# Sixteen more modulation steps placed after the recurrence, in three buffers, and attention's output projection begun in held banks

## The chip, the cores and the metric

The kernel runs on one core of one Trainium2 chip, as one launch. The metric is the device time of that core in microseconds, the median of several executions. Before the change three executions took 1273.87, 1274.51 and 1278.54 us, so the median is 1274.51 us.

## What is computed

One step of a two-layer streaming encoder over a prompt of 256 rows and a sample of 64 rows, each row 1024 wide, 320 columns together in the kernel's transposed layout. Cut to what matters:

```python
for l in range(2):
    mod = silu(c) @ ada_w[l] + ada_b[l]            # 1024 x 6144, one row per sequence
    sh1, sc1, g1, sh2, sc2, g2 = split(mod, 6)
    if l == 1:
        kvsh, kvsc = split(silu(c) @ kv_ada_w + kv_ada_b, 2)      # 1024 x 2048
        k, v = split(modulate(rmsnorm(x), kvsh, kvsc) @ w_kv)     # shared keys and values
    h = modulate(rmsnorm(x), sh1, sc1)
    y = rwkv7_time_mix(h) if l == 0 else window_attn(h, k, v)     # both end in a 1024 x 1024 projection
    x = x + g1 * y
    h = modulate(rmsnorm(x), sh2, sc2)
    x = x + g2 * hier_moe(h)                       # 32 experts of 1024 x 512 and 256 x 1024
y = rmsnorm(x)
```

The modulation vectors depend on `c` alone, so nothing but their first use says when they must be computed.

## The kernel before

The engines' programs are written by hand, each in its own order, with semaphores between them; a helper `Engine` counts what each engine did, and `wait` waits for a named piece of another engine's work. Nothing reorders: what stands later in an engine's program, or in SyncE's list of loads, can't overtake. All matmuls of a kind go through the helper `mm` (line 697), so most TensorE rows of the profile have that line.

**Modulation.** `MODS` (line 150) lists six groups of 2048 columns of `ada_w` or `kv_ada_w` beside the first one. A group is eight steps of 128 input rows; a step needs a load of 128 x 2048 values (1 MB), and is four matmuls of 512 columns against `cs` (`mod_rows`), which add up in one PSUM bank that is held over the group (`Banks.hold`, line 227). After the eighth step ScalarE copies the bank to a row buffer, TensorE transposes it (`mod_turn`, line 709), and VectorE adds the bias (`turned`, line 1564). Steps 0 to 31 (`EARLY = 4` groups, `MSTEPS = 32`) stand in the recurrence, steps 32 to 47 in attention (`late_step`, line 733). SyncE loads them in turn into two buffers (`mw`, `mw_late`), a load waiting until the step two before it has used its buffer.

**Recurrence** of layer 0 (time mixing), in chunks of 64 columns, 5 chunks. Part A (from line 889 on) computes per chunk the 64 x 64 products, and turns `v`, `b`, `k` to rows; one modulation step stands after the products and two after the turning (`A_STEPS = 3`). Then `for l in range(2, 7)` (line 914) inverts triangular matrices by five levels of doubling: per level five `W` products, then per chunk one `TW` product, which VectorE (lines 1707 to 1719) masks, adds and transposes, and which the next level's `W` needs. After the `TW` of chunks 0, 1, 2, 3 one modulation step each (`LEVEL_STEPS`, line 155). Then the state recursion, the normalisation of `y` (`head_sums`, `head_spread`), and the output projection `wo` (line 1006): eight outputs of eight matmuls each, whose inputs VectorE delivers one chunk at a time ("mix out").

**Prelude of the experts** (`moe`, line 1008): mean square, `keep_busy` (matmuls on constants into an unused bank), router logits, turning, ranks, gathering of rows; then a loop over the experts. SyncE's list in `moe_loads` (line 512) fills the ring's four slots.

**Attention** of layer 1 (loop at line 1242): stages s = 0 to 10 pipeline eight chunks; `project("q", [s])`, two late modulation steps, `mod_turn`, `prob_turn(s-3)`, `q_turn(s-1)`, `scores(s-2)`, `attended(s-3)`. In the tail (s = 8 to 10) there is no `q` and no modulation step. Then `project("ao", range(C), ...)` (line 1264) makes the eight outputs, then the second prelude and the second expert loop.

PSUM has eight banks, given out in turn by `Banks.open` (line 233), which leaves out held banks and waits until the bank's last owner has been read:

```python
        while self.n % 8 in self.held:
            self.n += 1
        ...
        if self.owner[b] is not None:
            self.pe.wait("read", *self.owner[b])
```

Of the kernel before, what the change touches and what calls it, by code (L numbers as in the profile page):

```python
# [36 lines left out]
P = 128  # L37
# [114 lines left out]
EARLY = 4  # L152
MSTEPS = C * EARLY
A_STEPS = 3
LEVEL_STEPS = (1, 1, 1, 1, 0)
# [89 lines left out]
def build(nc, i, o, known, seen):  # L245
    ctx = ExitStack()
    with ctx:
# [3 lines left out]
        def sem(name):  # L251
# [30 lines left out]
                                       "swkv_in", "router_in0", "router_in1", "out_written", "modw_in0", "modw_in1", "lora2_in")}  # L282
# [112 lines left out]
        modrow = [ring[:, 3 * B + 2048:3 * B + 2560], work[:, 6 * B:6 * B + 512]]  # L395
        mw_late = [ring[:, s_ * SLOT + 4096:(s_ + 1) * SLOT] for s_ in (2, 3)]
        modrow_late = work[:, 7 * B + 2048:8 * B]
# [87 lines left out]
        def _(eng):  # L485
# [25 lines left out]

            def moe_loads(l):
# [58 lines left out]
            def mod_load(n, dst):  # L571

                w, l, blk, _b = MODS[n // C]
                src = i[w] if l is None else i[w][l]
                eng.dma_start(dst, src[P * (n % C):P * (n % C) + P, 2048 * blk:2048 * (blk + 1)]
                              ).then_inc(in_sems[f"modw_in{n % 2}"], 16)

            for n in range(MSTEPS):
# [6 lines left out]
                mod_load(n, mw[n % 2])  # L585
# [10 lines left out]
            for n in range(MSTEPS, C * len(MODS)):  # L596
                if n >= MSTEPS + 2:
                    sp.wait("mod used", n - 2)
                mod_load(n, mw_late[n % 2])
# [91 lines left out]
        def _(eng):  # L691
# [17 lines left out]
            def mod_turn(g):  # L709
# [3 lines left out]
                for qd in range(4):  # L713
                    cols = slice(P * qd, P * qd + P)
                    ins = eng.transpose(pb[:, cols], (modrow_late if g >= EARLY else modrow[g < 0])[:, cols],
                                        ident)
                full(ins, "modT", g)

            def mod_step(n):
# [3 lines left out]
                if n < MSTEPS:  # L723
# [4 lines left out]
                    eng.wait_ge(in_sems[f"modw_in{n % 2}"], 16 * (n // 2 + 1))  # L728
                    pe.did(mod_rows(ps[seen_bank(("mod", g))], c, mw[n % 2]), ("mod used", n), ("mod", g))
# [3 lines left out]
            def late_step(n):  # L733
# [5 lines left out]
                eng.wait_ge(in_sems[f"modw_in{n % 2}"], 16 * (n // 2 + 1))  # L739
# [1339 lines left out]
```

## Time and profile before

| | |
|---|---|
| median of three runs | 1274.51 us |
| the profiled execution's own time | 1278.17 us |
| its span, first to last instruction | 1276.4 us |
| mean granted TensorE clock | 0.952 of full speed |
| TensorE matmul busy | 1130.6 us (89%) |
| VectorE busy | 541.1 us (42%) |
| ScalarE busy | 341.3 us (27%) |
| HBM read | 293.77 MB, 232 GB/s over the span |

The profiled execution is 3.66 us above the median, and its span 1.77 us below its own time. In the rows, PE is TensorE, PEld its weight loads, DVE VectorE, ACT ScalarE, SP SyncE; times are in us from the span's start, and a float32 matmul appears as two rows' worth of instructions, so a step of four matmuls counts as x8. A number in brackets is the time for which the engine stood idle before the row, with what ended it.

### The profile page before, as it was taken

The page shows a single profiled execution, that of the slowest core. Times are in us where ns is not written, and L with a number is a line of the kernel's source. Part 1 is how long each engine was busy: PE and PEld are TensorE (multiplying, and loading weights), DVE is VectorE, ACT ScalarE, POOL GpSimd, SP SyncE. Part 2 cuts the span into 40 slices and gives each one's busy share as a digit, 9 for nine tenths or more (in the row PEclk, how much of TensorE's full clock was granted, in tenths as well). Part 3 has the DMA queues.
Part 4 walks back from the last instruction along what each step waited for, and adds up shares of the span by engine and source line. Part 5 has one row for each costly group of instructions (what it writes and reads, how often), then busy time and mean ns, then how long its engine had stood idle before and what let it go on. Part 6 is the DMA issues. An engine that isn't in the chain of part 4 may idle for free.

```text
span 1276.4 us, 22255 instructions
## 1 busy us (share of the span) xinstructions
PE 1130.6 (89%) x8975; PEld 652.7 (51%) x8975; DVE 541.1 (42%) x1419; ACT 341.3 (27%) x650; POOL 56.3 (4%) x66
## 2 busy tenths in 40 slices
PE   5579998888888799999999989898899999999984
PEld 2146666656686556444444446455666444444433
DVE  3430366544522545244444444144346244444434
ACT  1112241112123012233333222233222233333312
POOL 2000000000000000001000000000000000010000
PEclk9589999998999799999999999999899999999997
DMA  9631313875632440399999964457250199999931
GB/s 238 197 132 66 132 66 108 281 257 193 232 135 64 175 190 1 138 415 426 425 427 424 423 236 186 160 209 280 91 198 1 65 425 420 426 427 424 426 152 41
DMA packets 45971, 297.11 MB, mean 233 GB/s; under 512 B 5956, under 2 KB 7336, under 8 KB 22344
## 3 DMA queue, kind: packets, MB, share of 16 engines
q1 hardware_dynamic: 43856, 290.17, 57.3%
q0 software_dynamic: 1840, 5.79, 2.0%
q8 instruction: 58, 0.95, 0.3%
q10 hardware_dynamic: 200, 0.06, 0.0%
q14 instruction: 17, 0.14, 0.0%
HBM read 293.77 MB, written 2.24 MB: 232 GB/s over the span
## 4 chain that ended last, share of the span: by engine, by line
PE 78%; DVE 9%; DMA 8%; ACT 2%; issue 2%; SPq 0%; ACTq 0%; DVEq 0%; POOL 0%; POOLq 0%
PE bank L697 76%; DMA ring<-in_ada_w 6%; DVE work L1545 2%; ACT work L1286 1%; DMA ring<-in_kv_ada_w 1%; DVE work L1551 1%; DVE work L1548 1%; DVE rstd L1583 1%; DVE x_res L1917 1%; DMA ring<-in_rw_w_rkv 1%; PE bank L1095 1%; DVE work L1903 1%; DVE ring L1545 1%; DVE work L1657 0%; PE bank L1215 0%
## 5 line engine op out<-in xcount | busy, mean ns | idle before, releaser
L697 PE MATMUL bank<-ring,work 128*64 128x512 f32 (+1 forms) x1600 | 341.2, 579 | 9.3 <-DVE work L1903 7.6
L697 PE MATMUL bank<-work,ring 128*128 128x320 f32 (+3 forms) x1600 | 302.5, 367 | 24.0 <-DVE work L1545 8.4
L697 PEld LDWEIGHTS bank<-work,ring 128*128 128x128 f32 (+2 forms) x1600 | 213.1, 172 | 112.3 <-issue 25.2
L697 PE MATMUL bank<-work 128*128 128x320 bf16 (+7 forms) x1906 | 225.3, 284 | 21.9 <-DVE x_res L1917 7.7
L697 PEld LDWEIGHTS bank<-ring,work 128*64 128x64 f32 (+1 forms) x1600 | 112.9, 137 | 210.7 <-issue 203.6
L697 PEld LDWEIGHTS bank<-work 128*128 128x128 bf16 (+3 forms) x1906 | 165.6, 126 | 93.6 <-issue 25.8
L1286 ACT ACTIVATE work<-bank 128x320 f32<-128x320 f32 (+6 forms) x113 | 57.0, 540 | 244.2 <-PE bank L697 218.6
L1917 DVE SCALAR_TENSOR_TENSOR x_res<-bank,mod,x_res 128x256 f32<-128x256 f32 (+1 forms) x256 | 86.1, 378 | 18.5 <-PE bank L697 4.8
L1897 DVE SCALAR_TENSOR_TENSOR work<-work,small,bank 128x256 f32<-128x256 f32 x32 | 21.5, 672 | 168.7 <-ACT work L1450 89.3
L697 PE MATMUL bank<-ring,cs 128*32 128x512 f32 x448 | 63.3, 656 | 31.5 <-DMA ring<-in_ada_w 23.9
L697 PEld LDWEIGHTS bank<-ring 64*64 64x64 f32 (+2 forms) x1984 | 71.8, 140 | 26.0 <-issue 23.8
L697 PE MATMUL bank<-ring 64*64 64x64 f32 (+2 forms) x1984 | 82.1, 232 | 3.4 <-issue 3.4
L1286 ACT ACTIVATE ring<-bank 128x512 f32<-128x512 f32 (+3 forms) x65 | 36.5, 561 | 151.4 <-PE bank L697 150.3
L1910 DVE TENSOR_TENSOR work<-bank,work 128x512 f32<-128x512 f32 x64 | 44.0, 688 | 61.9 <-ACT work L1454 61.9
L651 POOL TENSOR_TENSOR work<-work 128x512 bf16<-128x512 f32 x32 | 36.4, 1158 | 538.2 <-ACT work L1458 538.2
L1454 ACT ACTIVATE work<-bank 128x512 bf16<-128x512 f32 x64 | 38.1, 595 | 49.3 <-PE bank L697 49.3
L1551 DVE SCALAR_TENSOR_TENSOR work<-work,vec 128x320 f32<-128x320 f32 x56 | 27.0, 546 | 54.5 <-PE bank L697 54.2
L1438 ACT COPY work<-work 128x512 f32 x64 | 39.3, 623 | 14.2 <-issue 14.1
L1458 ACT ACTIVATE work<-work 128x512 bf16<-128x512 f32 x64 | 40.0, 626 | 8.6 <-DVE work L1910 8.6
L1286 ACT ACTIVATE work<-x_res 128x640 f32<-128x640 f32 x20 | 14.7, 737 | 99.9 <-DVE x_res L1551 46.5
L697 PEld LDWEIGHTS bank<-ring,cs 128*32 128x32 f32 x448 | 10.5, 112 | 56.7 <-DMA ring<-in_ada_w 30.6
L697 PE MATMUL bank<-const 128*128 128x320 f32 x122 | 37.9, 466 | 0.0
(189 smaller groups left out, 801.8 us busy)
## 6 DMA issues: line engine op xcount, KB each, us to landing
ring<-in_moe_w_gu SPq DMA_DIRECT2D x64, 2048.0 KB, 13.8
ring<-in_moe_w_down SPq DMA_DIRECT2D x64, 1024.0 KB, 14.6
ring<-in_ada_w SPq DMA_DIRECT2D x40, 1024.0 KB, 5.3
ring<-in_rw_w_rkv SPq DMA_DIRECT2D x6, 2048.0 KB, 7.9
ring<-in_ada_w SPq DMA_DIRECT2D x4, 2048.0 KB, 29.5
ring<-in_kv_ada_w SPq DMA_DIRECT2D x8, 1024.0 KB, 5.4
ring<-in_rw_w_o SPq DMA_DIRECT2D x2, 2048.0 KB, 11.9
ring<-in_at_w_q SPq DMA_DIRECT2D x2, 2048.0 KB, 14.1
```

Source lines behind the costliest of these rows:

```text
L651: eng.tensor_tensor(dpart[:, 0, 2, cols], rest[:, n, :], dpart[:, 0, 1, cols], ALU.subtract).then_inc(S["lo_ready0"], 1)
L697: return eng.matmul(out, l, r, start=start, stop=stop, **kw)
L1095: ins = eng.transpose(ps[0][:, 2 * P * u + P * f:2 * P * u + P * f + P], hid[:, u, P * f:P * f + P], ident)
L1286: ac.did(eng.activation(out, in_, f, **kw), *keys)
L1438: eng.copy(xe[:, u, :, 64 * v:64 * v + 64], xall[:, :, bass.ds(at, SLOTS)]).then_inc(S["xe_ready"], 1)
L1454: eng.activation(dpart[:, u, 0, 512 * n:512 * n + 512], ps[4 + n][:, :], ACT.Copy).then_inc(S["hi_ready"], 1)
L1458: eng.activation(dpart[:, u, 1, 512 * n:512 * n + 512], rest[:, n, :], ACT.Copy).then_inc(S["mid_ready"], 1)
L1545: op(eng.tensor_tensor(out, a, b, o_), *keys)
L1551: op(eng.scalar_tensor_tensor(out, a, s_, b, o1, o2), *keys)
L1897: eng.scalar_tensor_tensor(hid_w[:, u], silu[:, u, :].rearrange("p (q f) -> p q f", f=2), wslot[:, u:u + 1], ps[3 + 4 * u][:, FE:2 * FE].r ...
L1910: eng.tensor_tensor(rest[:, n, :], ps[4 + n][:, :], dpart[:, u, 0, 512 * n:512 * n + 512], ALU.subtract).then_inc(S["rest_ready"], 1)
L1917: ins = eng.scalar_tensor_tensor(x[:, c, t0:t0 + n], ps[(6, 1, 2)[c % 3]][:, t0:t0 + n], mod[:, l, r, 40 + c:40 + c + 1], x[:, c, t0:t0 + ...
```

## The change

Steps 16 to 31 (groups 2 and 3: the shared keys' modulation, and shift and scale of layer 1) leave the recurrence, and `MIDDLE = 4` marks where they end. In the recurrence part A keeps two steps per chunk, and the levels two of four (after the `TW` of chunks 0 and 2), so that the sixteen that are left are done by level 4. Step 16 goes behind the sum of `yc` squares, step 17 behind the spread of `y rstd`, steps 18 to 25 behind one output each of `wo`, 26 to 28 and 29 to 31 into the first prelude, where `keep_busy` has 13 matmuls less (7, 9 and 6 become 1, 3 and 5). Their loads go into three buffers in `work`, and into SyncE's list at four places of `moe_loads(0)`. The third buffer is where `bonus` lay, so its first load waits for the last "mix out". A copy on ScalarE and two additions on VectorE per group move with them, and a memset of `xall`'s tail, whose place the buffers take, goes behind them.

In attention, three of the eight outputs of `ao` get banks that are held from stage 8 on; their partial products over chunks 0 to 3 stand at the head of stage 8, chunks 4 and 5 at the head of stage 9, chunk 6 behind the loop, chunk 7 inside the fourth output. The number of matmuls is the same.

```diff
-EARLY = 4
+EARLY = 2
 MSTEPS = C * EARLY
-A_STEPS = 3
-LEVEL_STEPS = (1, 1, 1, 1, 0)
+A_STEPS = 2
+LEVEL_STEPS = (1, 0, 1, 0, 0)
+MIDDLE = 4
...
+        mw_middle = [work[:, a:a + 2048] for a in (B, 3 * B, 2 * B)]
...
+            def middle_loads(steps):
+
+                for n in steps:
+                    if n == MSTEPS + 2:
+                        sp.wait("mix out", PAIRED[-1])
+                    elif n > MSTEPS + 2:
+                        sp.wait("mod used", n - 3)
+                    mod_load(n)
+
             def moe_loads(l):
...
                     sp.wait("y all")
+                    middle_loads(range(MSTEPS, MSTEPS + 2))
                     eng.wait_ge(in_sems["out_written"], 64)
                     moe_gu(l, 2, 2)
                     moe_dn(l, 2, 2)
                     moe_gu(l, 3, 3)
                     sp.wait("y rstd all", PAIRED[-1])
                     moe_dn(l, 3, 3)
+                    middle_loads(range(MSTEPS + 2, MSTEPS + 9))
                 for s in ((0, 1) if l == 0 else (0, 1, 3, 2)):
+                    if l == 0 and s == 1:
+                        middle_loads(range(MSTEPS + 9, MSTEPS + 13))
...
+                if l == 0:
+                    middle_loads(range(MSTEPS + 13, MSTEPS + 16))
...
             head_sums("yc sum", E[0], "yc squares")
+            late_step(MSTEPS)
             pe.wait("y rstd")
             head_spread("y rstd all", heads)
-            project("wo", range(C), rr, lambda hf: ("wo", hf), ("mix out",))
+            late_step(MSTEPS + 1)
+            for m in range(C):
+                project("wo", [m], rr, lambda hf: ("wo", hf), ("mix out",))
+                if m == C - 1:
+                    mod_turn(EARLY)
+                late_step(MSTEPS + 2 + m)
...
                 mean_square(f"B{l}")
-                keep_busy(7)
+                if l == 0:
+                    for n in range(MSTEPS + 10, MSTEPS + 13):
+                        late_step(n)
+                keep_busy(7 if l else 1)
...
-                keep_busy(9)
+                if l == 0:
+                    for n in range(MSTEPS + 13, MSTEPS + 16):
+                        late_step(n)
+                    bank.held.clear()
+                keep_busy(9 if l else 3)
                 pe.wait("mask", l)
...
-                keep_busy(6)
+                if l == 0:
+                    mod_turn(EARLY + 1)
+                keep_busy(6 if l else 5)
...
+            def out_part(cs_):
+
+                for m in range(3):
+                    if m not in part:
+                        arrived(pe, "ao", 0)
+                        part[m] = bank.hold("ao", m)
+                for c in cs_:
+                    pe.wait("oT", c)
+                    for m in range(3):
+                        ins = mm(part[m][:, 0:T], w512(3)[:, c, 128 * m:128 * m + 128], oT[:, c, :], c == 0,
+                                 c == C - 1)
+                        if c == C - 1:
+                            full(ins, "ao", m)
+
             for s in range(C + 3):
+                if s == C:
+                    bank.held.clear()
+                    out_part(range(4))
+                if s > C:
+                    out_part([4, 5] if s == C + 1 else [])
...
-            project("ao", range(C), oT, lambda hf: ("ao", hf), ("oT",))
+            out_part([6])
+            pb = bank.open("ao", 3)
+            for c in range(C):
+                if c == C - 1:
+                    out_part([c])
+                ins = mm(pb[:, 0:T], w512(3)[:, c, 384:512], oT[:, c, :], c == 0, c == C - 1)
+            pe.did(ins, ("ao", 3), ("used", "ao", 0))
+            bank.held.clear()
+            project("ao", range(4, C), oT, lambda hf: ("ao", hf), ("oT",))
...
             def squares(tag):
                 for b in range(4):
+                    if tag == "B0" and b == 2:
+                        act(modrow_of(EARLY), pk("mod", EARLY)[:, :], ACT.Copy, ("read", "mod", EARLY),
+                            ("mod rows", EARLY))
...
+                if l == 0:
+                    late_turned(EARLY + 1)
+                    ve.wait("mod used", C * MIDDLE - 1)
+                op(eng.memset(xall[:, :, ROWS:RP], 0.0))
```

The line numbers shift, so that `mm` is line 728 in the changed kernel, `mod_turn`'s transposes line 746, and `prob_turn`'s lines 1262 and 1267. In the rows of order, `x` counts the matmuls as they are written.

TensorE, one level of the doubling and the next level's start, in the kernel before (64x64 are the `W` and `TW` products, 16 each; `ring,cs` a modulation step):

```order
L697 MATMUL bank<-ring,cs 32x512 x4
L697 MATMUL bank<-ring 64x64 x112
L697 MATMUL bank<-ring,cs 32x512 x4
L697 MATMUL bank<-ring 64x64 x16
L697 MATMUL bank<-ring,cs 32x512 x4
L697 MATMUL bank<-ring 64x64 x16
L697 MATMUL bank<-ring,cs 32x512 x4
L697 MATMUL bank<-ring 64x64 x16
L697 MATMUL bank<-ring,cs 32x512 x4
L697 MATMUL bank<-ring 64x64 x112
```

and in the changed one:

```order
L728 MATMUL bank<-ring,cs 32x512 x4
L728 MATMUL bank<-ring 64x64 x128
L728 MATMUL bank<-ring,cs 32x512 x4
L728 MATMUL bank<-ring 64x64 x32
L728 MATMUL bank<-ring,cs 32x512 x4
L728 MATMUL bank<-ring 64x64 x128
```

Two of the four steps of a level have gone, and between the two that are left stand two `TW` products on one side, and on the other two `TW`, five `W` and one `TW`.

TensorE from the sum of `yc` squares to the first outputs of `wo`, in the kernel before (`ring,const_phase` is the spread, `work,ring` the projection's 64 matmuls):

```order
L697 MATMUL bank<-work,const 32x320 x8
L697 MATMUL bank<-ring,const_phase 128x320 x8
L697 MATMUL bank<-work,ring 128x320 x64
L697 MATMUL bank<-work,const 128x320 x8
L697 MATMUL bank<-const 128x320 x7
```

and in the changed one (`work,cs` is a modulation step from the new buffers), the first rows and the last ones:

```order
L728 MATMUL bank<-work,const 32x320 x8
L728 MATMUL bank<-work,cs 32x512 x4
L728 MATMUL bank<-ring,const_phase 128x320 x8
L728 MATMUL bank<-work,cs 32x512 x4
L728 MATMUL bank<-work,ring 128x320 x8
L728 MATMUL bank<-work,cs 32x512 x4
...
L728 MATMUL bank<-work,ring 128x320 x8
L746 MATMUL bank<-const,work 128x128 x4
L728 MATMUL bank<-work,cs 32x512 x4
L728 MATMUL bank<-work,const 128x320 x8
L728 MATMUL bank<-work,cs 32x512 x12
L728 MATMUL bank<-const 128x320
```

A step stands behind each output, and behind the last one also a turn, ahead of the mean square (`work,const 128x320`).

TensorE in attention from the last modulation step's stage on, with the banks' numbers, in the changed kernel (bank 3 was held by modulation group 5 until there; `work,ring 128x320` is the output's part):

```order
L728 MATMUL bank3<-ring,cs 32x512 x8
...
L728 MATMUL bank2<-work 64x64 x16
L728 MATMUL bank3<-work,ring 128x320
L728 MATMUL bank4<-work,ring 128x320
L728 MATMUL bank5<-work,ring 128x320
...
L1262 MATMUL bank6<-const,work 128x128 x4
L1267 MATMUL bank7<-const,work 64x128 x4
L728 MATMUL bank0<-work,const_phase 128x320
```

Between `attended(4)` (bank 2) and the turn of chunk 5's probabilities (bank 6), where nothing stood before, there are now twelve matmuls into banks 3, 4 and 5.

## Rows read from the trace of the kernel before

**Rows 1.** Page, part 4: the chain that ended last, by engine.
```profile
PE 78%; DVE 9%; DMA 8%; ACT 2%; issue 2%; SPq 0%; ACTq 0%; DVEq 0%; POOL 0%; POOLq 0%
```

**Rows 2.** Waits of TensorE, 205 to 470 us: total us, times, longest.
```profile
PE bank L697 <- DMA ring<-in_ada_w: 12.7, 9, 2.3
...
PE bank L697 <- DMA ring<-in_kv_ada_w: 6.5, 4, 2.1
```

**Rows 3.** Timeline of TensorE in the recurrence: start, duration, operation, idle before.
```profile
212.66 5.15 PE L697 MATMUL bank<-work,ring 64*64 64x128 f32 x64 [2.83 <-DVE work L1545]
...
224.88 3.71 PE L697 MATMUL bank<-work,ring 64*64 64x128 f32 x64
228.52 1.06 PE L697 MATMUL bank<-ring,cs 128*32 128x512 f32 x8
229.51 1.15 PE L697 MATMUL bank<-const,work 64*64 64x64 f32 x32
230.49 2.03 PE L697 MATMUL bank<-const,ring 64*64 64x64 f32 x64
...
235.33 1.07 PE L697 MATMUL bank<-ring,cs 128*32 128x512 f32 x8 [1.81 <-DMA ring<-in_ada_w]
...
271.94 5.81 PE L697 MATMUL bank<-ring 64*64 64x64 f32 x192
...
357.87 1.10 PE L697 MATMUL bank<-const,ring 64*64 64x64 f32 x32
```

**Rows 4.** Timeline of VectorE, the first two chunks of a level.
```profile
277.88 0.69 DVE L1545 TENSOR_TENSOR ring<-ring,const_phase 128x512 f32<-128x512 f32 x1 [9.34 <-PE bank L697]
278.49 0.68 DVE L1545 TENSOR_TENSOR ring<-ring,bank 128x512 f32<-128x512 f32 x1
...
279.88 0.69 DVE L1545 TENSOR_TENSOR ring<-ring,const_phase 128x512 f32<-128x512 f32 x1
```

**Rows 5.** Stretches: length; busy PE, PEld, DVE, ACT, POOL; granted clock; DMA share; GB/s.
```profile
259.00:262.00 3.00, 3.00 (x36) 2.45 (x30) 0.76 (x2) 0.00 (x0) 0.00 (x0) 0.67 0.90 300
...
889.00:893.00 4.00, 4.00 (x22) 2.90 (x24) 1.01 (x3) 1.19 (x2) 0.00 (x0) 0.50 0.96 406
893.00:897.00 4.00, 4.00 (x64) 3.10 (x60) 1.75 (x6) 0.76 (x5) 0.00 (x0) 0.76 1.05 446
...
888.88:909.04 20.16, 16.29 (x166) 12.49 (x166) 7.45 (x31) 8.50 (x30) 0.00 (x0) 0.67 0.57 239
909.04:945.23 36.19, 36.19 (x131) 25.46 (x130) 9.00 (x21) 2.65 (x4) 0.00 (x0) 0.96 0.22 87
```

**Rows 6.** Timelines of TensorE and VectorE around the output projection of layer 0.
```profile
416.42 1.97 PE L697 MATMUL bank<-ring,const_phase 32*128 32x320 f32 x16 [3.27 <-DVE ring L1734]
...
429.48 0.49 DVE L1545 TENSOR_TENSOR work<-work 128x320 f32<-128x320 f32 x1
432.03 0.68 DVE L1551 SCALAR_TENSOR_TENSOR x_res<-bank,mod,x_res 128x256 f32<-128x256 f32 x2 [2.06 <-PE bank L697]
436.34 0.68 DVE L1551 SCALAR_TENSOR_TENSOR x_res<-bank,mod,x_res 128x256 f32<-128x256 f32 x2 [3.63 <-PE bank L697]
```

**Rows 7.** Page, part 6: loads, count, KB each, median us to landing.
```profile
ring<-in_moe_w_gu SPq DMA_DIRECT2D x64, 2048.0 KB, 13.8
...
ring<-in_ada_w SPq DMA_DIRECT2D x40, 1024.0 KB, 5.3
```

**Rows 8.** First prelude: a wait of TensorE, and when the experts' first matmuls ran.
```profile
PE bank L697 <- DVE work L1824: 2.2, 1, 2.2
...
523.28 7.11 PE bank L697 x32
```

**Rows 9.** Timelines of attention's tail: TensorE, ScalarE, and VectorE's last output.
```profile
888.88 1.11 PE L1215 MATMUL bank<-const,work 128*128 128x128 f32 x4 [4.17 <-DVE work L1548]
...
887.10 0.62 ACT L1286 ACTIVATE work<-bank 128x512 f32<-128x512 f32 x1
...
945.23 0.80 DVE L1548 TENSOR_SCALAR work<-bank,mod,bog 128x256 f32<-128x256 f32 x2 [2.99 <-PE bank L697]
```

More of the change, by code:

```diff
@@ L394, in build, with modrow_of, mod_at @@
         mw = [ring[:, 3 * B:3 * B + 2048], ring[:, tail3:tail3 + 2048]]
-        modrow = [ring[:, 3 * B + 2048:3 * B + 2560], work[:, 6 * B:6 * B + 512]]
         mw_late = [ring[:, s_ * SLOT + 4096:(s_ + 1) * SLOT] for s_ in (2, 3)]
-        modrow_late = work[:, 7 * B + 2048:8 * B]
+        mw_middle = [work[:, a:a + 2048] for a in (B, 3 * B, 2 * B)]
+        modrows = {"first": work[:, 6 * B:6 * B + 512], "early": ring[:, 3 * B + 2048:3 * B + 2560],
+                   "middle": work[:, B + 2048:2 * B], "late": work[:, 7 * B + 2048:8 * B]}
+        def modrow_of(g):
+            return modrows["first" if g < 0 else "early" if g < EARLY else "middle" if g < MIDDLE else "late"]
+        def mod_at(n):
+            if n < MSTEPS:
+                return mw[n % 2], f"modw_in{n % 2}", 16 * (n // 2 + 1)
+            m = n - MSTEPS
+            if n < C * MIDDLE:
+                return mw_middle[m % 3], f"modm_in{m % 3}", 16 * (m // 3 + 1)
+            return mw_late[n % 2], f"modw_in{n % 2}", 8 * MSTEPS + 16 * ((n - C * MIDDLE) // 2 + 1)
         lows = {"w": ring[0:64, tail3:tail3 + T], "a": ring[64:128, tail3:tail3 + T],
@@ L595, in _ @@
                 half(name, w, hf)
-            for n in range(MSTEPS, C * len(MODS)):
-                if n >= MSTEPS + 2:
+            for n in range(C * MIDDLE, C * len(MODS)):
+                if n >= C * MIDDLE + 2:
                     sp.wait("mod used", n - 2)
-                mod_load(n, mw_late[n % 2])
+                mod_load(n)
             half(("ao", 1), i["at_w_o"][0], 1)
@@ L1302, in mod_copy @@
                     ac.wait("modT", g - 1)
-                    act(modrow[0], pb[:, :], ACT.Copy, ("read", "mod", g), ("mod rows", g))
+                    act(modrow_of(g), pb[:, :], ACT.Copy, ("read", "mod", g), ("mod rows", g))
             ac.wait("rows zeroed")
@@ L1321, in _ @@
             root("A0")
-            act(modrow[1], pk("mod", -1)[:, :], ACT.Copy, ("read", "mod", -1), ("mod rows", -1))
+            act(modrow_of(-1), pk("mod", -1)[:, :], ACT.Copy, ("read", "mod", -1), ("mod rows", -1))
             modulated("A0", h0, h0)
@@ L1423, in moe @@
                 act(rt[:, 36, 0:3], rt[:, 35, 0:3], ACT.Exp, ("route exp", l))
+                if l == 0:
+                    g = EARLY + 1
+                    pb = pk("mod", g)
+                    ac.wait("modT", EARLY)
+                    act(modrow_of(g), pb[:, :], ACT.Copy, ("read", "mod", g), ("mod rows", g))
                 for hf in range(2):
@@ L1507, in _ @@
                 if s in (4, C):
-                    g = EARLY + (s == C)
-                    act(modrow_late[:, :], pk("mod", g)[:, :], ACT.Copy, ("read", "mod", g), ("mod rows", g))
+                    g = MIDDLE + (s == C)
+                    act(modrow_of(g), pk("mod", g)[:, :], ACT.Copy, ("read", "mod", g), ("mod rows", g))
                 if s >= 3:
@@ L1757, in moe @@
                 eng.wait_ge(in_sems["out_written"], (64, 144)[l])
-                op(eng.memset(xall[:, :, ROWS:RP], 0.0))
                 op(eng.tensor_tensor_scan(count640[:, :], cst("ones")[:, 0:1].broadcast_to([P, ROWS]),
```

54 lines of the change are left out of this document (30 added, 24 removed).

## The prediction, made before the changed kernel was run

> **What bounds the kernel now.** I read the chain of waits first: 78% of the span it runs through TensorE, and 8% through DMA [rows 1]. So two questions decide this change: where does TensorE wait, and does moved work land where it waited anyway? TensorE's waits between 205 and 470 us give the first answer. It stood 12.7 and 6.5 us, 19.2 in all, for loads of modulation weights [rows 2], and all of that lies in the recurrence. The timeline shows how: a step is 0.99 us (228.52 to 229.51), with three per chunk, and the third finds its load not there (1.81 us at 235.33) [rows 3]. Next I read who is second: VectorE in the levels [rows 4]. Then the stretches that take the moved work: the projection of layer 0, where VectorE waits for TensorE 3.63 us per output [rows 6], so TensorE is the bound there, and attention's tail, where TensorE pauses 4.17 us in one piece [rows 9].
>
> **Part A of the recurrence.** A chunk without its waits is 3.64 us of products (224.88 to 228.52), 0.98 and 2.03 us of turning, and its steps [rows 3]. With two steps that is 3.64 + 0.98 + 2.03 + 1.98 = 8.6 us, so five chunks take 43.0; the first one's products take 1.4 longer (5.15 for 3.71), a turn 0.6: 45.0 us, for 271.94 - 212.66 = 59.3 now. **Minus 14.3.** Do the loads keep up? A buffer comes free when its step is done, and is wanted one chunk of 8.6 us less one step later, 7.6 us; a load lands after 5.3 us [rows 7]. They do.
>
> **The levels.** They take 357.87 - 271.94 = 85.9 us [rows 3]. Ten products of 16 x 2 instructions are 5.81 / 6 = 0.97 us each, 9.7 us a level; with two steps 11.7. VectorE needs 2.0 us per chunk (277.88 to 279.88), 10.2 a level at 2.05, and becomes second: after its fifth chunk's add (0.69 + 0.68 us in) the last `W` and the next `TW` must run, 1.94, and two hand-overs of some 0.2, while only 0.7 of transposing is left [rows 4]. So a level has a floor of 10.2 + 1.7 = 11.9 us on VectorE too. Taking 12.0: 5.8 to the first `TW`, four periods, four products: 5.8 + 48.0 + 3.9 = 57.7, which saves 28.2. I take 1.4 off for pauses in which TensorE waits for nothing shown, "issue", 2% of the chain [rows 1]. **Minus 26.8.** Bounds for the whole recurrence: at least the sixteen steps' own 16 us and half the load waits, 9.6, so 25.6; at most 14.3 + 28.2 = 42.5, where nothing is lost.
>
> **Where the steps go.** Steps 16 and 17 cost nothing: their loads start when `y` is done, and they run at about 413 and 418 us, where TensorE waits for VectorE's reciprocal (3.27 us at 416.42) and then for the inputs of `wo`, the last of which comes at 429.97 [rows 6]. Without that cover they would cost 2.0.
>
> Steps 18 to 25 stand between the outputs of `wo`, which follow each other at 4.31 us (432.03 to 436.34) on a full TensorE [rows 6]: nothing hides them. **Plus 8.0**, and the turn behind the last one **plus 0.6**.
>
> Step 18 has a new wait. Its buffer is `bonus`, so its load, and those of 19 and 20 behind it in SyncE's list, wait for the last "mix out" at 429.97 [rows 6], and land 5.3 us later, at 435.3 [rows 7]. Output 0 is done at 431.9, so TensorE stands 3.4 us with seven outputs queued behind the step. **Plus 3.4** (bounds: 0, if the load were as quick as the 2.06 us VectorE waits there; 11.9, if it took the 13.8 of an expert load with others ahead). The next loads have two periods, 10.6 us, and don't wait.
>
> The DMA page of the Trainium skill, "DMA: Bandwidth & Descriptors", section Bandwidth, gives 6.15 us for 1 MB, measured on the POOL queue; by it the stall would be 4.3 and the sum 0.9 more. The trace's 5.3 is of these loads on this queue, and decides.
>
> Such a pause also costs clock. After the longest of the waits for loads, 2.3 us [rows 2], the granted clock at 259 to 262 was 0.67; after the 4.17 us in attention 0.50, the lower of the two levels (1.2 of 2.4 GHz), for 4 us and 0.76 for 4 more [rows 5]. That is (1 - 0.67) x 3 = 1.0 us lost at least, and 4 x 0.50 + 4 x 0.24 = 3.0. The stall of 3.4 lies nearer the second. **Plus 2.5**, bounds 1.0 and 3.0.
>
> Steps 26 to 31 take the place of 13 `keep_busy` matmuls of 0.54 us, 7.0 us, with 6 x 0.99 and a turn of 0.6: 6.5. They stand ahead of waits for VectorE (2.2 us for the mask) [rows 8], so even a late load is covered. Their loads share the queue with the experts' slots 0 and 1, issued some 15 us later than now with the rest of the program, at 13.8 us to landing [rows 7]; the first matmuls that need those come at 523.28 [rows 8], 60 us after the projection. ScalarE's two copies (0.62 us as at 887.10 [rows 9]) and VectorE's additions and memset, under 1 us a group, go where both engines wait for TensorE. **Zero**; if that cover failed, 1 to 2 us.
>
> **Attention's tail.** Now TensorE stands from 884.71 to 888.88, when the probabilities of chunk 5 are ready [rows 9]. The twelve matmuls, 12 x 0.54 = 6.5 us, are meant for that pause. But clearing the held banks lets the first of them open bank 3, which belonged to modulation group 5; ScalarE reads that one at 887.10 to 887.72 [rows 9]. So the pause shrinks to 3.1 us only, still costs clock, and everything behind the twelve (the last `q_turn`, `scores`, probabilities) starts near 897 where it was 888.88. What follows took 20.16 us until the projection, 16.29 of it busy at 0.67 clock, and then 36.19 at 0.96 [rows 5]: at full clock 10.9 and 34.7. Best case: no pause, 887.75 + 10.9 + 34.7 = 933.4 for 945.23, a gain of 11.9. Worst: the 20.16 repeat and the clock loses 3.0: 887.75 + 6.5 + 3.0 + 20.16 + 36.19 - 6.5 = 947.1, a loss of 1.9. My walk: the twelve end at 897; 10.9 of work, six matmuls of chunks 4 and 5 at 3.2 us, which lie where TensorE waited for probabilities, and 1.7 of pauses bring 912.8; the 46 matmuls left are 24.8: 937.6. **Minus 7.6.** It is nearer the best case, because the work behind the twelve is denser and so keeps its clock.
>
> **Sum.** -14.3 - 26.8 + 8.0 + 0.6 + 3.4 + 2.5 - 7.6 = -34.2 us. On the profiled execution's 1278.17 that is 1244.0. The median of the runs shown is 3.66 lower, 1274.51, and my forecast is for it: **1240.3 us**.
>
> **The rivals.**
> 1. *The recurrence keeps waiting.* The two steps left in a level come close together, so loads may still be late, or TensorE's own supply of instructions shows up. For it: these waits hold 19.2 us today, and pauses without a semaphore exist. Against it: a buffer has a whole period of 12 us. It gives the lower bound, 25.6 for 41.1: 1255.8. Chance 0.10.
> 2. *Attention gives nothing.* The twelve only push the softmax chain back. For it: the chain through `q_turn`, `scores` and ScalarE's exponentials is serial, and starts 8 us later. Against it: 18 matmuls, 9.7 us, are gone from the end. 1247.9. Chance 0.12.
> 3. *No stall, no clock lost.* Load 18 is there early enough and the tail comes near its best: -42.5 + 8.6 + 1.0 - 11.0 = -43.9, 1230.6. Against it is the row at 429.97. Chance 0.12.
> 4. *Slower: TensorE at its lower level through the whole projection.* If every step from 18 on waits for its load, the clock never recovers: eight outputs of 4.31, eight steps and the mean square's 4.3 take twice as long, some 47 us more, less the 2.5 already counted, so 1240.3 + 44.5 = 1284.8. It decides once a load takes two periods of 5.3 and a wait like the 2.3 us one in the recurrence, 12.9 us. The loads of 2 MB with others queued ahead take 13.8, those of 1 MB 5.3 [rows 7]. The Trainium skill, "TensorE: Matmul & The Clock Gate", section HAM oscillation, describes just that: a group of matmuls shorter than the wait for its next load starts cold each time. Here the rule bears on step 18, whose price stands above from rows; the others have 10.6 us for a load of 5.3. Chance 0.02.
> 5. *The steps move, but their cost moves with them*, each load wait turning up in the projection: 1274 +- 5. Chance 0.02.
>
> **How the numbers follow.** My forecast has 0.62. Its own range, with the recurrence at 38 to 42.5, the clock at 1.0 to 3.0 and the tail at 4 to 11, is 1234 to 1248. Reaching to rivals 2 and 3 gives **1230 to 1251**; left out are rivals 1, 4, 5 and some of 3's lower half, 0.18. About 0.5%, 6.4 us, is what a measurement here can tell from no change. Faster: 0.62 + 0.10 + 0.12 + 0.12 = 0.96; same 0.02; slower 0.02.
>
> **What would show it.** In the changed profile: part A near 45 us and no wait for `ada_w` there; a level's period near 12 us; a stall of 3 to 4 us for `work<-in_kv_ada_w` once, behind the first output of `wo`, and a granted clock near 0.5 to 0.7 behind it; VectorE's residual adds at 5.3 us, not 4.31; in attention a pause of 3 us ended by ScalarE before the first `ao` part, and 46 matmuls behind the last `attended`. I am wrong if waits for loads stay in the levels, if more than one step of the projection waits, or if the tail's gain is under 4 us.

## The result, and the profile after

The changed kernel took 1238.57 us (median of four runs, 1234.86 to 1241.91) for 1274.19 us of the kernel before beside it (four runs, 1272.28 to 1278.54): a recorded ratio of 0.9726, 95% interval 0.9687 to 0.9765 (the recorded ratios differ a little from the quotients of the medians, 0.9720 here). The forecast was 1240.3 in 1230 to 1251. The profiled execution took 1236.46 us, its span is 1234.7 us, and its mean granted clock 0.968 of full speed.

The page of the changed kernel gives the chain by engine, and the first group of the moved steps' loads (steps 16 to 23: count, KB each, median us to landing).

```profile
PE 80%; DVE 10%; DMA 5%; ACT 2%; issue 2%; SPq 0%; ACTq 0%; DVEq 0%; POOL 0%; POOLq 0%
...
work<-in_kv_ada_w SPq DMA_DIRECT2D x8, 1024.0 KB, 5.6
```

DMA's share of the chain went from 8% to 5% [rows 1]. These are the first of TensorE's waits in the changed kernel between 205 and 470 us (total us, times, longest):

```profile
PE bank L728 <- DVE work L1627: 5.6, 2, 2.8
PE bank L728 <- DMA work<-in_kv_ada_w: 3.9, 1, 3.9
PE bank L728 <- issue: 3.9, 3, 1.7
```

The 19.2 us of waits for modulation loads [rows 2] have become one of 3.9. This is the timeline of TensorE over the recurrence, to be read against [rows 3]:

```profile
211.72 5.06 PE L728 MATMUL bank<-work,ring 64*64 64x128 f32 x64 [2.84 <-DVE work L1627]
...
256.54 6.10 PE L728 MATMUL bank<-ring 64*64 64x64 f32 x192
...
285.10 2.08 PE L728 MATMUL bank<-ring 64*64 64x64 f32 x63 [1.04 <-issue]
...
301.18 6.08 PE L728 MATMUL bank<-ring 64*64 64x64 f32 x192
308.03 5.81 PE L728 MATMUL bank<-ring 64*64 64x64 f32 x192 [0.77 <-DVE ring L1627]
313.68 1.10 PE L728 MATMUL bank<-const,ring 64*64 64x64 f32 x32
```

Part A takes 256.54 - 211.72 = 44.8 us where it took 59.3, and the levels 313.68 - 256.54 = 57.1 where they took 85.9. The timeline of VectorE shows where each of the five levels starts, to be read against [rows 4]:

```profile
262.75 0.69 DVE L1627 TENSOR_TENSOR ring<-ring,const_phase 128x512 f32<-128x512 f32 x1 [6.82 <-PE bank L728]
...
274.31 0.69 DVE L1627 TENSOR_TENSOR ring<-ring,const_phase 128x512 f32<-128x512 f32 x1 [1.75 <-PE bank L728]
...
287.22 0.69 DVE L1627 TENSOR_TENSOR ring<-ring,const_phase 128x512 f32<-128x512 f32 x1 [3.04 <-PE bank L728]
...
298.84 0.69 DVE L1627 TENSOR_TENSOR ring<-ring,const_phase 128x512 f32<-128x512 f32 x1 [1.76 <-PE bank L728]
...
310.16 0.69 DVE L1627 TENSOR_TENSOR ring<-ring,bank 128x512 f32<-128x512 f32 x1 [1.44 <-PE bank L728]
```

The periods are 11.6, 12.9, 11.6 and 11.3 us; the long one holds a pause of TensorE of 1.04 us (at 285.10) that waits for nothing shown. The first three levels have two steps each. The fourth has none, and yet is only 0.3 us shorter: there TensorE waits 0.77 us for VectorE (at 308.03).

This is the output projection of layer 0 in TensorE's timeline:

```profile
381.31 5.73 PE L728 MATMUL bank<-work,ring 128*128 128x320 f32 x14 [2.78 <-DVE work L1627]
390.97 1.07 PE L728 MATMUL bank<-work,cs 128*32 128x512 f32 x8 [3.93 <-DMA work<-in_kv_ada_w]
391.97 6.26 PE L728 MATMUL bank<-work,ring 128*128 128x320 f32 x16
398.16 1.06 PE L728 MATMUL bank<-work,cs 128*32 128x512 f32 x8
399.15 4.57 PE L728 MATMUL bank<-work,ring 128*128 128x320 f32 x16
403.66 1.06 PE L728 MATMUL bank<-work,cs 128*32 128x512 f32 x8
404.65 4.57 PE L728 MATMUL bank<-work,ring 128*128 128x320 f32 x16
```

The stall stands where it was forecast, behind the first output, at 3.93 us; the output behind it takes 6.26 us where the later ones take 4.57, so the clock costs 1.7 us. Later outputs follow each other at 5.50 us (399.15 to 404.65). Attention's tail, to be read against [rows 9], is shown for TensorE, then ScalarE, then VectorE's last output.

```profile
858.22 6.70 PE L728 MATMUL bank<-work,ring 128*128 128x320 f32 x24 [3.11 <-issue]
...
866.26 4.06 PE L728 MATMUL bank<-work 64*64 64x64 f32 x72
...
878.84 1.30 PE L728 MATMUL bank<-work 128*64 128x64 f32 x32 [0.72 <-ACT work L1360]
880.07 25.03 PE L728 MATMUL bank<-work,ring 128*128 128x320 f32 x92
```

```profile
857.50 0.62 ACT L1360 ACTIVATE work<-bank 128x512 f32<-128x512 f32 x1
```

```profile
905.14 0.80 DVE L1630 TENSOR_SCALAR work<-bank,mod,bog 128x256 f32<-128x256 f32 x2 [2.98 <-PE bank L728]
```

The pause is 3.11 us, from 855.11, and ends as ScalarE has read group 5's bank (858.12), though the view calls it "issue". From the pause's start to the last output passed 945.23 - 884.71 = 60.5 us before, and 905.14 - 855.11 = 50.0 now. These are the stretches with their granted clock (the number ahead of the DMA share and GB/s), to be read against [rows 5]:

```profile
256.54:313.68 57.14, 55.25 (x1657) 49.08 (x1654) 41.39 (x66) 15.54 (x26) 0.00 (x0) 1.00 0.29 95
391.00:395.00 4.00, 4.00 (x14) 2.18 (x15) 0.00 (x0) 0.00 (x0) 0.00 (x0) 0.63 1.01 426
395.00:399.00 4.00, 4.00 (x19) 2.05 (x18) 0.68 (x2) 0.02 (x1) 0.00 (x0) 0.95 0.64 268
858.00:862.00 4.00, 3.78 (x14) 2.77 (x15) 1.19 (x6) 0.12 (x1) 0.00 (x0) 1.00 0.93 395
...
880.07:905.14 25.07, 25.07 (x97) 17.77 (x94) 8.75 (x21) 2.65 (x4) 0.00 (x0) 1.00 0.32 126
```

The levels ran at 1.00 and TensorE was busy in them 97% of the time. Behind the stall the clock was 0.63; behind attention's pause it was 1.00 in this execution.

From profile to profile the kernel is 41.7 us shorter, from median to median 35.6. The profile before is of one of its longest executions (1278.17). Part A (-14.5), the levels (-28.8), the projection (+14.7, worked out below) and the tail (-10.5) make -39.1 of the -41.7; the rest is spread over stretches that the change doesn't touch, such as the shared keys' matmuls, 19.15 us in the profile before and 17.47 here.

### The profile page after: what moved, and what is told of

Its sections match the earlier page's. It is cut to its first block, busy times and chain, and to the rows that moved or that the text cites. A ratio compares the mean times of both kernels' runs of the same rounds, so it can differ in the third digit from the quotient of the medians.

```text
span 1234.7 us, 22208 instructions
## 1 busy us (share of the span) xinstructions
PE 1108.7 (90%) x8949; PEld 637.3 (52%) x8949; DVE 539.8 (44%) x1419; ACT 340.7 (28%) x650; POOL 56.4 (5%) x66
## 4 chain that ended last, share of the span: by engine, by line
PE 80%; DVE 10%; DMA 5%; ACT 2%; issue 2%; SPq 0%; ACTq 0%; DVEq 0%; POOL 0%; POOLq 0%
PE bank L728 78%; DMA ring<-in_ada_w 4%; DVE work L1627 2%; ACT work L1360 2%; DVE work L1633 1%; DVE ring L1627 1%; DVE rstd L1665 1%; DVE x_res L2012 1%; DMA ring<-in_rw_w_rkv 1%; DVE work L1630 1%; PE bank L1142 1%; DVE work L1998 1%; DVE work L1739 0%; PE bank L1346 0%; DMA work<-in_kv_ada_w 0%
## 5 line engine op out<-in xcount | busy, mean ns | idle before, releaser
L728 PEld LDWEIGHTS bank<-work,ring 128*128 128x128 f32 (+2 forms) x1600 | 208.5, 168 | 117.5 <-issue 32.9
L728 PE MATMUL bank<-work 128*128 128x320 bf16 (+7 forms) x1906 | 222.2, 279 | 22.9 <-DVE x_res L2012 7.7
L728 PEld LDWEIGHTS bank<-work 128*128 128x128 bf16 (+3 forms) x1906 | 163.1, 122 | 91.5 <-issue 23.8
L728 PE MATMUL bank<-ring 64*64 64x64 f32 (+2 forms) x1984 | 78.1, 227 | 1.9 <-issue 1.0
L728 PEld LDWEIGHTS bank<-ring 64*64 64x64 f32 (+2 forms) x1984 | 69.1, 136 | 15.3 <-issue 12.1
L728 PE MATMUL bank<-ring,cs 128*32 128x512 f32 x320 | 43.2, 638 | 13.9 <-DMA ring<-in_ada_w 12.8
L1360 ACT ACTIVATE work<-x_res 128x640 f32<-128x640 f32 x20 | 14.7, 736 | 91.3 <-DVE x_res L1633 49.1
L1975 DVE TENSOR_SCALAR work<-const,work 128x64 bf16<-128x64 f32 x192 | 32.7, 249 | 4.4 <-PE bank L728 4.2
L1530 ACT ACTIVATE work<-bank 128x320 bf16<-128x320 f32 x32 | 12.2, 434 | 80.1 <-PE bank L728 80.1
```

Of the source, the lines that this page charges most:

```text
L728: return eng.matmul(out, l, r, start=start, stop=stop, **kw)
L1360: ac.did(eng.activation(out, in_, f, **kw), *keys)
L1975: ins = eng.tensor_scalar(sel[:, u, j, a], cst("iota"), posn[:, j, bass.ds(e + v, 1)], None, ALU.is_equal, ALU.bypass)
```

## Experiments

The table has every run; "before" is the kernel before, run beside it on the same chip. In the expectations T1 is the prediction's own theory, T2 and T3 are theories added to it, and R1 to R8 are their rivals.

| run | median us (range) | before | ratio, 95% interval |
|---|---|---|---|
| a0_after, the changed kernel | 1239.45 (1238.39 to 1241.44) | 1274.29 | 0.9736 (0.9701 to 0.9771) |
| e1_no_ao | 1249.18 (1246.63 to 1252.86) | 1274.29 | 0.9812 (0.9774 to 0.9850) |
| e3_buffer18 | 1236.20 (1232.50 to 1239.66) | 1274.29 | 0.9703 (0.9666 to 0.9741) |
| e4_bank | 1234.55 (1233.34 to 1235.36) | 1274.29 | 0.9696 (0.9661 to 0.9730) |
| e2_ao_only | 1265.70 (1262.65 to 1267.44) | 1272.79 | 0.9932 (0.9906 to 0.9957) |
| e5_busy | 1237.95 (1235.96 to 1241.40) | 1272.79 | 0.9724 (0.9697 to 0.9751) |
| e6_no_loads | 1248.81 (1246.56 to 1252.01) | 1272.79 | 0.9811 (0.9785 to 0.9838) |
| e7_early | 1232.86 (1231.43 to 1235.80) | 1272.79 | 0.9685 (0.9659 to 0.9711) |
| e8_best | 1226.90 (1223.91 to 1229.43) | 1275.47 | 0.9637 (0.9598 to 0.9676) |
| a1_after, the changed kernel | 1241.28 (1238.25 to 1243.47) | 1275.47 | 0.9747 (0.9707 to 0.9786) |
| e9_level5 | 1222.89 (1220.50 to 1225.14) | 1272.77 | 0.9602 (0.9573 to 0.9630) |
| e8_again | 1226.87 (1216.75 to 1228.76) | 1272.77 | 0.9628 (0.9602 to 0.9655) |

**The changed kernel again**, as the number beside which the variants on its chip are read (a0_after, later a1_after).

> The changed kernel itself, beside which the variants sent with it are to be read, on the same chip. The prediction's theory (T1: TensorE's load waits and the clock they cost go from the recurrence, ten steps move into full TensorE time behind it, attention's tail gains 7 to 10): 34 to 37 us under the kernel before, 1236 to 1241. No other theory says anything else of a repeat.

> The changed kernel itself, on the same chip as the combination, as the number that it is compared with: 1236 to 1241.

The first came out as expected, the second 0.3 us above its range.

**Was it the waits, or the steps' own time?** This is the kernel before, with the loads of steps 2 to 31 left out, and with them the right values of these vectors:

```diff
-                mod_load(n, mw[n % 2])
+                if n < 2:
+                    mod_load(n, mw[n % 2])
...
```

> The kernel before, with the loads of modulation steps 2 to 31 left out: these steps compute on the two buffers that were loaded once, so TensorE does the same matmuls in the same order and waits for no modulation load in the recurrence. It leaves out 30 loads of 1 MB and with them the right values of these vectors. It parts the gain of the change in the recurrence (43 us in the profiles) into waits and their clock on one side and the steps' own TensorE time on the other. T1: the 19.2 us of waits go, and some 4 to 6 us of clock behind them; part A from 59.3 to about 50 to 51, the levels from 85.9 to about 69 to 71: 22 to 26 us faster than the kernel before, so that the steps' own 16 to 20 us are the smaller half of the gain. Rival R5 (the steps' own TensorE time is nearly all, the waits turn into other waits, for VectorE or in TensorE's own sequencer): under 10 us faster.

It measured 24.0 us under the kernel before. Its timeline of TensorE:

```profile
209.15 6.57 PE L698 MATMUL bank<-work,ring 64*64 64x128 f32 x64 [2.83 <-DVE work L1546]
...
259.77 5.82 PE L698 MATMUL bank<-ring 64*64 64x64 f32 x192
...
327.79 1.10 PE L698 MATMUL bank<-const,ring 64*64 64x64 f32 x32
```

Part A takes 50.6 us and the levels 68.0 (1 us under the expected 69 to 71), together 118.6 where the kernel before took 145.2. So the waits and their clock were 26.6 us of the 43.3 that the change takes out of the recurrence (145.2 - 102.0); the sixteen steps' own time is the other 16.7. The split rests on one profile of each kernel: here the first row took 6.57 us for 5.15 before and 5.06 after, so some 1.5 us of the 118.6 is another clock at the start, and without it the waits' share is larger still. R5 falls.

**Step 18's stall.** Its load goes where the finished `y`'s last piece lay, so that it need not wait for the last "mix out":

```diff
+                if m == 2:
+                    return work[:, 5 * B:5 * B + 2048], "modm_in2", 16
...
-                    if n == MSTEPS + 2:
+                    if n == MSTEPS + 5:
                         sp.wait("mix out", PAIRED[-1])
-                    elif n > MSTEPS + 2:
+                    if n > MSTEPS + 2:
                         sp.wait("mod used", n - 3)
...
-                    middle_loads(range(MSTEPS, MSTEPS + 2))
+                    middle_loads(range(MSTEPS, MSTEPS + 3))
...
-                    middle_loads(range(MSTEPS + 2, MSTEPS + 9))
+                    middle_loads(range(MSTEPS + 3, MSTEPS + 9))
```

> The change, with step 18's load put where the finished y's last piece lay, so that it needs not wait for the last inputs of the output projection and is issued with the loads of 16 and 17; the wait for those inputs now stands ahead of step 21's load. T1: the stall of 3.9 us behind the first output of wo goes, and the 1.7 us of clock lost after it: 4.5 to 6 us faster than the changed kernel, no wait over 1 us for a modulation load behind it. Rival R2 (the stall only moves to the next step whose buffer waits, step 19 or 21, or the time is lost again in the experts' prelude): within 2 us of the changed kernel, with a wait for a modulation load of 2 us or more at a later step.

The stall goes, and no later step waits for its load, so R2's mechanism is not there. TensorE in this kernel:

```profile
383.04 6.95 PE L730 MATMUL bank<-work,ring 128*128 128x320 f32 x14 [2.74 <-DVE work L1629]
389.92 1.06 PE L730 MATMUL bank<-work,cs 128*32 128x512 f32 x8
390.91 4.57 PE L730 MATMUL bank<-work,ring 128*128 128x320 f32 x16
```

From the spread's start to the experts' first matmul it takes 492.30 - 374.19 = 118.1 us, the changed kernel's repeat 496.23 - 372.52 = 123.7: 5.6 less, as expected. By medians it is 3.3 less, under the expected range. In the repeat the same place looks like this, first in SyncE's queue, then in TensorE:

```profile
386.05 22.16 SPq L532 DMA_DIRECT2D work<-in_kv_ada_w  x6
```

```profile
394.07 1.93 PE L728 MATMUL bank<-work,cs 128*32 128x512 f32 x8 [5.71 <-DMA work<-in_kv_ada_w]
395.93 5.39 PE L728 MATMUL bank<-work,ring 128*128 128x320 f32 x16
```

The same stall is 5.71 us here, since the load issued at 386.05 is used at 394.07, after 8.0 us; in the changed kernel's first profile it was used after 5.0 us (issued at 386.00, used at 390.97). In four more executions with this code the stall was 5.01, 5.18, 5.38 and 6.37.

What lay ahead of it was an expert's load. The rows give that load's issue, its time to landing, and the times to landing of the loads of steps 18, 19 and 20, first in the repeat, then in the first profile:

```profile
375.43 0.33 SPq L523 DMA_DIRECT2D ring<-in_moe_w_down  x1
DMA to landing us min/median/max: 13.5/13.5/13.5
DMA to landing us min/median/max: 8.0/10.1/12.0
```

```profile
375.38 0.33 SPq L523 DMA_DIRECT2D ring<-in_moe_w_down  x1
DMA to landing us min/median/max: 12.3/12.3/12.3
DMA to landing us min/median/max: 4.9/7.0/9.0
```

In the repeat the expert's load landed 2.9 us after step 18's was issued (375.43 + 13.5 against 386.05), and step 18's landed 5.1 us behind it; in the first profile it was 1.7 and 3.2. The four other executions have 2.3 to 2.8 and 4.9 to 5.2. So the load waited for the one ahead of it; why only 3.2 us followed in one execution stays open.

**Steps 17 to 20 in TensorE's wait** ahead of the projection, with their loads ahead of the experts' and step 18's other buffer as above:

```diff
-            late_step(MSTEPS + 1)
+            for n in range(MSTEPS + 1, MSTEPS + 5):
+                late_step(n)
...
-                late_step(MSTEPS + 2 + m)
+                if m >= 3:
+                    late_step(MSTEPS + 2 + m)
```

> Step 18's load in the finished y's place as before, and also the loads of steps 19 and 20 ahead of the experts' loads, and steps 17 to 20 together behind the spread, where TensorE waits about 6 us for the first inputs of the output projection; only steps 21 to 25 stay behind outputs of wo. T1 (what is hidden in a wait costs nothing, what stands between full outputs costs its 1.0 us, and the stall its 3.9 and 1.7): 7 to 10 us faster than the changed kernel. Rival R6 (the inputs of wo come as late, but the four steps' loads or the experts' loads behind them come later, and TensorE waits there instead): 2 to 5 us faster at most, with a wait for a load at one of steps 18 to 20 or at an expert.

```profile
375.98 5.35 PE L730 MATMUL bank<-work,cs 128*32 128x512 f32 x24
382.81 1.07 PE L730 MATMUL bank<-work,cs 128*32 128x512 f32 x8 [1.49 <-DMA work<-in_kv_ada_w]
383.81 17.49 PE L730 MATMUL bank<-work,ring 128*128 128x320 f32 x64
```

TensorE does the four steps here, the last one waiting 1.49 us for its load, and then four outputs back to back at 4.37 us each. The same stretch as above takes 487.71 - 373.27 = 114.4 us, 9.3 less than the repeat's. By medians it is 39.9 under its kernel before, the repeat 34.8 under its own: 5.1 us (6.6 between the two medians themselves). So the place pays as T1 says, and the total falls short of 7 to 10. In the two profiles the rest lies behind, where the code is the same: from the second prelude's mean square to the end the repeat has 327.1 us and this kernel 329.7, 2.6 more. That stretch is 327.0 to 327.2 in three of the profiles here and 329.6 to 331.4 in all others, whatever the kernel; what makes it shorter in some executions is not shown.

**Attention's part taken out, and alone.** It is taken out of the change (the edit below), and then added to the kernel before without the moved steps:

```diff
-                    out_part(range(4))
-                if s > C:
-                    out_part([4, 5] if s == C + 1 else [])
...
-            out_part([6])
...
-            project("ao", range(4, C), oT, lambda hf: ("ao", hf), ("oT",))
+            project("ao", range(C), oT, lambda hf: ("ao", hf), ("oT",))
```

> The change with its attention part undone: all eight outputs of attention's projection again behind the loop, sixteen steps moved as in the change. T1, with the tail's 10.5 us as the profiles show it: 7 to 11 us slower than the changed kernel, about 1246 to 1249, and the pause before the last chunks back at 4.2 us with a granted clock near 0.5 to 0.7 behind it. Rival R1 (the tail's gain in the profile is only another phase of the clock in that execution, the twelve matmuls push the softmax chain back by as much as they save): within 3 us of the changed kernel.

> The kernel before with attention's part of the change alone, all thirty-two early modulation steps left in the recurrence. T1: 7 to 11 us faster than the kernel before, about 1263 to 1267, recurrence unchanged. Rival R1 (no gain in attention by itself): within 3 us of the kernel before.

It is worth 9.7 us on the changed kernel (1249.18 - 1239.45) and 7.1 on the kernel before (1272.79 - 1265.70). Both lie in the expected 7 to 11, and R1 falls. This is the pause in the changed kernel without the part:

```profile
860.78 1.12 PE L1262 MATMUL bank<-const,work 128*128 128x128 f32 x4 [4.18 <-DVE work L1619]
```

and in the kernel before with it:

```profile
887.24 8.09 PE L697 MATMUL bank<-work,ring 128*128 128x320 f32 x24 [3.11 <-issue]
```

**Group 5's bank held on**, so that the parts' banks are others:

```diff
-                    bank.held.clear()
+                    old = set(bank.held)
                     out_part(range(4))
+                    bank.held -= old
```

> The change, with modulation group 5's bank kept held until the three banks of attention's output are taken, so that the first of them needs not wait for ScalarE's copy of that bank. T1: the pause of 3.1 us before the first of these matmuls goes or shrinks under 0.5 us, and the end comes 2 to 3.5 us earlier. Rival R3 (the chain of probabilities on ScalarE and VectorE sets the tail, and TensorE will stand as long before the turn of chunk 5's probabilities): the pause reappears there, and the time is within 1 us of the changed kernel.

```profile
855.01 6.73 PE L728 MATMUL bank<-work,ring 128*128 128x320 f32 x24
```

In this kernel the twelve matmuls start with no pause, and none appears behind them. It is 4.9 us faster by medians, more than the 2 to 3.5 expected; R3 falls. What was probably missing in the expectation shows in the repeat of the changed kernel and in the kernel with step 18's other buffer:

```profile
861.09 8.39 PE L728 MATMUL bank<-work,ring 128*128 128x320 f32 x24 [3.11 <-issue]
```

```profile
854.19 9.57 PE L730 MATMUL bank<-work,ring 128*128 128x320 f32 x24 [3.10 <-issue]
```

The pause is always 3.1 us, but the same twelve matmuls behind it take 6.70, 8.09, 8.39 or 9.57 us: the clock costs 0 to 2.9 us more, and differs between executions.

**Fillers of the first prelude put back** (`keep_busy` 7, 9 and 6 in both layers):

```diff
-                keep_busy(7 if l else 1)
+                keep_busy(7)
...
-                keep_busy(9 if l else 3)
+                keep_busy(9)
...
-                keep_busy(6 if l else 5)
+                keep_busy(6)
```

> The change with the first prelude's thirteen removed filler matmuls on constants put back (7, 9 and 6 where the change has 1, 3 and 5). Theory T2 (the first prelude became 1.2 us longer because the router's logits run at a lower clock, having fewer fillers ahead of them): the logits' matmuls back near 4.0 us for 5.2, the prelude shorter, 0 to 2 us faster than the changed kernel. Rival R4 (the moved steps fill TensorE as the fillers did and the fillers now push work back): 3 to 7 us slower, thirteen times 0.54 us at most.

It is 34.8 us under its kernel before, just as the changed kernel's repeat: no effect that these runs can tell, and not the 3 to 7 us of R4. T2's reason falls too: from VectorE's mean square to the experts' first matmul the first profile of the changed kernel has 57.9 us (the kernel before 56.7), and its repeat 55.9 with no edit at all.

**The best of these together**: early steps and held bank.

> The two edits that measured faster, together: steps 17 to 20 and their loads early (6.5 us under the changed kernel by medians, 8.9 in the profile's stretch) and group 5's bank kept held until attention's output has its three banks (4.9 us). T1 (the two stand in different places and add up): about 11 us under the changed kernel, 1226 to 1230, no pause over 0.5 us ahead of attention's output and no wait for a modulation load over 2 us behind the projection's first output. Rival R7 (what one saves the other's clock gives back): no faster than the better of the two, 1232 to 1235.

It is 14.4 us under the changed kernel on its chip (1226.90 for 1241.28), where the two alone gave 6.6 and 4.9 by the same kind of difference. So the two add up, and R7 falls; no run shows where the other 2.9 us come from.

**Two steps from part A into the fourth level**, on top of it:

```diff
-A_STEPS = 2
+A_STEPS = (2, 2, 2, 1, 1)
...
-    first = A_STEPS * NCH + sum(LEVEL_STEPS) * (l - 2)
+    first = sum(A_STEPS) + sum(LEVEL_STEPS) * (l - 2)
...
```

> The combination, with one modulation step less in each of part A's last two chunks, and two more in the fourth of the five levels, which has none in the changed kernel: there TensorE stood 0.77 us for VectorE at the level's end, and the period was 11.3 us where levels with two steps have 11.6. T3 (a level without steps is bound by VectorE, so two steps in it cost about 0.3 together, while in part A a step costs its 1.0): part A from 44.8 or 46.3 to 2.0 less, that level 0.2 to 0.5 longer, the recurrence 1.5 to 1.8 shorter than the combination's 102.8 in the profile; by medians 0 to 3 us, hardly to be told. Rival R8 (TensorE is the bound there too): the level becomes 2 us longer, the recurrence the same.

> The combination itself, on the same chip as the variant sent with it: 1224 to 1230.

VectorE of this variant, at the start of the fourth and of the fifth level:

```profile
294.24 0.69 DVE L1637 TENSOR_TENSOR ring<-ring,const_phase 128x512 f32<-128x512 f32 x1 [1.75 <-PE bank L735]
305.86 0.69 DVE L1637 TENSOR_TENSOR ring<-ring,bank 128x512 f32<-128x512 f32 x1 [1.76 <-PE bank L735]
```

Its period is 11.62 us with two steps, and 11.32 without them in the combination's second profile: 0.3 more, as T3 says, so R8 falls. The recurrence as a whole is not the 1.5 to 1.8 shorter that was expected: without its first group of matmuls, whose clock differs, it takes 95.9 us for 96.3; of what is missing, pauses that wait for nothing shown (0.95 and 0.37 us, for one of 0.77) explain half a microsecond. The medians are 4.0 apart; with runs of the combination from 1216.75 to 1228.76 and intervals that overlap, the size stays open, and so does whether it is faster at all. It has the lowest median of the kernels tried.

## Why the prediction was right, step by step

- **The bound**: right. TensorE's waits for modulation loads and their clock were the larger part of the gain in the recurrence, 26.6 of 43.3 us (e6_no_loads), and the moved steps cost TensorE's time except where a wait hides them (e7_early).
- **Part A**: 45.0 forecast, 44.8 measured, without a load wait.
- **The levels**: -26.8 forecast, -28.8 measured. The term that was mis-sized is "Taking 12.0": the period is 11.6, with one pause of 1.04 for the 1.4 allowed. That VectorE is the second bound was right: the level without steps takes 11.3 us, a little under the floor of 11.9, and two steps put into it cost 0.3 us (e9_level5).
- **Steps 16 and 17 at nothing**: right. No row of waits names their loads, and from the sum of squares in TensorE to the last "mix out" it took 20.2 us before, 20.8 in the first profile after and 20.2 in its repeat.
- **Steps 18 to 25**: "plus 8.0" was too little. Each costs the difference of 5.50 between outputs and the 4.31 of [rows 6], 1.19 us, or 9.5 in all, though the step's own row has 1.0.
- **The stall**: 3.4 forecast, 3.93 in the profile, 5.0 to 6.4 in five other executions. Both numbers that it was taken from were off. "and land 5.3 us later" is the median landing of the recurrence's loads [rows 7]; here an expert's load was still in flight when step 18's was issued (DMA share 1.00 and 0.99 from 375 to 385 in the first profile), and step 18's landed after 7.2 to 8.0 us in those five executions. In the first profile it landed after 4.9, and there the other number made the stall longer: output 0 was done 1.0 us after the last input, and not 1.9. The 6.15 us that the Trainium skill gives for 1 MB ("DMA: Bandwidth & Descriptors", section Bandwidth) made the stall 4.3; that is nearer to what was measured, but the load took 6.15 us in no execution here.
- **The clock behind it**: 2.5 forecast, 1.7 measured, and 1.7 to 2.7 in the five other executions, in the bounds. All later outputs ran at full clock and no further step of the projection waited, so rival 4 did not come up. The Trainium skill, "TensorE: Matmul & The Clock Gate", section HAM oscillation, describes groups of matmuls that are each shorter than the wait for the next load, so that each starts cold. Here one wait came, the clock fell once, and no run shows a repetition.
- **Projection as a whole**: from the last "mix out" to the mean square 36.6 us before and 51.3 now, +14.7 for 14.5 forecast. That it fits so well is luck in part: the steps were forecast too cheap and the clock too dear. The measured terms (9.5, 0.6, 3.9 and 1.7) make 15.7, and the first output, done 1.0 us sooner after its last input than before (1.1 for 2.06 to VectorE's first residual add), takes 1.0 off.
- **First prelude at zero**: 57.9, 55.9 and, with fillers, 56.6 us, for 56.7 before. That is zero, within what executions differ by.
- **Attention**: -7.6 forecast; -7.1 and -9.7 by the two runs, -10.5 in the profiles. The pause of 3.1 us and its cause were right, and e4_bank shows it. That the pause "still costs clock" held in some executions and not in the profiled one.
- **The total**: -34.2 forecast, -35.6 by medians, but -39.1 for the same places by the profiles. The profile before is 4.0 us above its kernel's median and the one after 2.1 below, and which stretches hold these 6.1 us is not shown. So the terms are known to about that much, and that the forecast lies within 1.7 us of the median is luck in part.
- **Rivals**: 1 and 5 fall by the waits' view, 2 by e1_no_ao and e2_ao_only. 3 did not happen, but it looked in the right place: with the stall and the pause taken away, e8_best measures 1226.9, lower still than the 1230.6 of that rival; there steps moved under a wait too.

## What to carry to other kernels

A step that waits for its load costs its own time, the wait, and the clock behind the wait: price the three apart, and move first the steps whose loads are late. A load that is issued behind others takes longer to land than the median of the same load elsewhere (here 7.2 to 8.0 us in five of six executions, for 5.3), so ask what is in flight when its buffer comes free. When work is put into an engine's pause, look at which buffer its first instruction opens: a bank whose last reader is late brings part of the pause back (here 3.1 us of 4.17), and holding it on was here worth 4.9 us.

## What the runs showed that was not expected

- The clock behind one and the same pause of 3.1 us differs between executions: the twelve matmuls took 6.70 us twice and 8.39 once in three executions of the changed kernel itself, 8.09 and 9.57 in variants whose attention is the same. So a single profile can be 3 us off in one such place, and the medians of five or more runs were needed.
- A modulation step of 1.0 us between outputs of 4.37 us lengthens their period by 1.1 to 1.2 us.
- The landing of one load of 1 MB behind the same loads took 4.9 and 8.0 us in two executions of one kernel.
